# Split-pair projections: five additions into PSUM banks in place of three copies, a join and four additions; evictions read PSUM; order of sums, shifts and loads changed

## The reference

```python
proj = h @ w_in                                   # 1024 x 15 thousand odd columns
branch = jnp.einsum('bsmw,mwd->bsmd', ys, w_branch)
merged @ w_out
u = causal_dwconv(h @ w_up, conv_w, conv_b)       # 3 taps, in front of silu(gate) * value
```

## Time and profile before

| | |
|---|---|
| median of 3 runs | 3483.22 us (3481.16 to 3489.34) |
| the profiled execution | 3483.49 us |
| its span in the profile | 3481.7 us |
| TensorE busy | 3194.5 us, 92% |
| VectorE busy | 1530.1 us, 44% |
| GpSimd busy | 949.2 us, 27% |
| ScalarE busy | 666.8 us, 19% |

### The profile page before, as it was taken

One profiled execution on the slowest core, in us unless ns is written; L12 is line 12 of the kernel. 1 busy time (PEld: TensorE's weight loads), 2 busy tenths in 40 slices (PEclk: granted clock), 3 DMA queues, 4 the chain that ended last, 5 costly groups with the idle time before them and its releaser, 6 DMA issues. The chain is left out here.

```text
span 3481.7 us, 54338 instructions
## 1 busy us (share of the span) xinstructions
PE 3194.5 (92%) x22920; PEld 2164.9 (62%) x22920; DVE 1530.1 (44%) x2308; ACT 666.8 (19%) x1332; POOL 949.2 (27%) x664
## 2 busy tenths in 40 slices
PE   8998999989999789988889999989979986999998
PEld 6855866974887578656555444468758854444432
DVE  4744646135454467445777403554344334011112
ACT  2233141111111333111000001111353211100001
POOL 1201223110222444212999470011365410000000
PEclk9999999998999899999999999989999968999999
DMA  4211223220231000042335342122210013899996
GB/s 156 83 31 41 81 85 103 79 67 0 87 119 49 2 3 4 32 144 74 115 115 156 124 126 66 55 73 73 81 42 3 3 43 133 326 406 409 409 409 256
DMA packets 120560, 406.11 MB, mean 117 GB/s; under 512 B 13824, under 2 KB 18560, under 8 KB 120064
## 3 DMA queue, kind: packets, MB, share of 16 engines
q1 hardware_dynamic: 113408, 377.47, 30.9%
q0 software_dynamic: 6912, 25.17, 2.3%
HBM read 398.39 MB, written 4.19 MB: 116 GB/s over the span
## 5 line engine op out<-in xcount | busy, mean ns | idle before, releaser
L712 PE MATMUL ps<-arena 128*128 128x256 f32 x4592 | 1024.9, 385 | 49.7 <-issue 18.2
L712 PEld LDWEIGHTS ps<-arena 128*128 128x128 f32 x4592 | 883.0, 193 | 202.2 <-issue 64.6
L752 PE MATMUL ps<-arena 128*128 128x512 f32 (+1 forms) x912 | 370.8, 565 | 23.8 <-DVE arena L1047 17.5
L752 PEld LDWEIGHTS ps<-arena 128*128 128x128 f32 x912 | 177.0, 196 | 210.9 <-issue 197.6
L665 POOL TENSOR_TENSOR arena<-arena 128x256 f32<-128x256 f32 x72 | 59.2, 822 | 730.2 <-ACT arena L837 730.2
L3357 PE MATMUL ps<-arena 128*64 128x512 f32 x1024 | 239.3, 602 | 4.9 <-PE ps L3387 2.6
L642 POOL TENSOR_TENSOR arena<-arena 128x512 f32<-128x512 f32 x72 | 92.7, 1287 | 500.6 <-DMA arena<-in_w_in 262.8
L429 PE MATMUL ps<-arena 128*128 128x512 f32 (+1 forms) x416 | 187.5, 611 | 28.8 <-DVE arena L1050 14.9
L837 ACT ACTIVATE arena<-ps 128x256 f32<-128x256 f32 x246 | 92.2, 383 | 586.0 <-PE ps L712 579.2
L3506 POOL TENSOR_SCALAR arena<-arena,small 128x1024 f32<-128x1024 f32 x64 | 188.3, 2942 | 9.3 <-DMA arena<-in_w_mod 5.4
L957 DVE TENSOR_TENSOR arena<-ps,arena 128x256 f32<-128x256 f32 x82 | 34.8, 425 | 351.4 <-PE ps L712 345.1
(11 more groups left out here) (432 smaller groups left out, 4268.1 us busy)
## 6 DMA issues: line engine op xcount, KB each, us to landing
arena<-in_w_in SPq DMA_DIRECT2D x166, 512.0 KB, 3.6
arena<-in_w_gate SPq DMA_DIRECT2D x128, 512.0 KB, 11.2
arena<-in_w_up SPq DMA_DIRECT2D x128, 512.0 KB, 15.0
arena<-in_w_down SPq DMA_DIRECT2D x128, 512.0 KB, 9.1
arena<-in_w_mod POOLq DMA_DIRECT2D x48, 512.0 KB, 4.3
arena<-in_ffn_up SPq DMA_DIRECT2D x44, 512.0 KB, 4.1
arena<-in_w_branch SPq DMA_DIRECT2D x32, 512.0 KB, 3.6
arena<-in_w_out SPq DMA_DIRECT2D x16, 512.0 KB, 3.9
```

The costliest lines, as they stand in the source:

```text
L712: last = nc.tensor.matmul(k.bank(b)[:, 0:HT], lhs[:, q * P:(q + 1) * P], rhs[:, q, :], start=(first and q == 0), stop=(q == 3), skip_group ...
L752: last = nc.tensor.matmul(out[0:j["m"], 0:j["n"]], w[:, q * m:(q + 1) * m], j["rhs"](q), start=(n == 0), stop=(n == kn - 1))
```

## The change

In a pair, only P1 is still copied (into c1). VectorE makes five additions: Q = P6 + P1 into c1; U3 = P7 + Q into c7; C22 = P5 + U3, written into the second half of the bank that P7 holds; C12 = (P5 + P3) + Q, written into the second half of the bank of P1 and P2; C21 = (P7 + P4) + Q, in place. So each job ends as 512 columns of one bank, and `finish` reads PSUM. P3, which TensorE adds to P5, now waits for C22, which reads P5. The join, the copy of C11 and the staging planes go. `finish` of job 0 runs before C21. Banks are handed on after other events: that of P6 after Q, of P5 and P3 after C12, and the two others after the jobs' evictions. ScalarE now evicts its jobs from PSUM in each case, where a plain copy was a no-op.

The order of VectorE: after a split unit's C22, the early sums of the next split unit are made if it is among the next three units, not only if it is the next. In the second block's input phase `finish` and the side step come before the sums, and the four steps of the turn are spread over units 17 to 20. GpSimd makes S1 and S3 of pair after pair with no join between. The shift of a norm is added by ScalarE. The fifteen spare loads are issued at the end of SP's work in the router's phase, behind the following loads.

```diff
-            free += [(b, (k.st_asm, asm0 + 4 * ns + 1)), (a, (k.st_cop, cop0 + 4 * ns + 4)),
-                     (c, (k.st_asm, asm0 + 4 * ns + 2)), (d, (k.st_asm, asm0 + 4 * ns + 3))]
+            free += [(b, (k.st_asm, asm0 + 5 * ns + 1)), (c, (k.st_asm, asm0 + 5 * ns + 4)), (a, jobs[i]["evac"]), (d, jobs[i + 1]["evac"])]
...
     def raw(u, m):
-        j = jobs[u["i"] + m]
-        return j["dst"] if j["eng"] == "A" else k.pl(h.staging[m])
+        return k.bank(u["banks"][("P2", "P4")[m]][0])
...
-                for u in splits:
-                    later = splits[u["s"] + 1] if u["s"] + 1 < ns else None
-                    join(pool, nc.gpsimd, u)
-                    if later:
-                        sum_op(pool, nc.gpsimd, later, "S1", k.st_sump)
-                        sum_op(pool, nc.gpsimd, later, "S3", k.st_sump)
+                for u in splits[1:]:
+                    sum_op(pool, nc.gpsimd, u, "S1", k.st_sump)
+                    sum_op(pool, nc.gpsimd, u, "S3", k.st_sump)
...
-                pe.wait_ge(*copied(u, "P5"))
+                pe.wait_ge(*put_together(u, "C22"))
                 pe.wait_ge(*summed(u, "S4"))
                 halved(u, "P3", plane(u, "S4"), h.x(st, 1, 1), first=False).then_inc(k.piece_done, 1)
-                pe.wait_ge(*copied(u, "P7"))
...
+                for v in units[ui + 1:ui + (4 if u["kind"] == "S" else 2)]:
+                    if v["kind"] == "S" and v["s"] not in summed_units:
+                        later = v
+                        summed_units.add(v["s"])
+                        break
                 if u["kind"] == "C":
+                    if side is not None:
+                        finish(u, 0)
+                        side.dve(dve, u["i"])
+                        if 17 <= ui < 21:
+                            started.add(0)
+                            turn(0, ui - 17)
                     if later:
                         sums_early(later)
                         sums_late(later)
-                    finish(u, 0)
-                    if side is not None:
-                        side.dve(dve, u["i"])
+                    if side is None:
+                        finish(u, 0)
                     continue
...
                 nc.vector.tensor_tensor(h.c1, bank("P6"), h.c1, ALU.add).then_inc(k.st_asm, 1)
+                dve.wait_ge(*put_together(u, "Q"))
+                nc.vector.tensor_tensor(h.c7, bank("P7"), h.c1, ALU.add).then_inc(k.st_asm, 1)
+                dve.wait_ge(*put_together(u, "U3"))
+                nc.vector.tensor_tensor(raw(u, 1)[:, HT:T], bank("P5"), h.c7, ALU.add).then_inc(k.st_asm, 1)
                 if later:
                     sums_early(later)
...
                 nc.vector.tensor_tensor(raw(u, 0)[:, HT:T], bank("P3"), h.c1, ALU.add).then_inc(k.st_asm, 1)
                 if later:
                     sums_late(later)
+                finish(u, 0)
                 dve.wait_ge(*closing(u, "P4"))
                 nc.vector.tensor_tensor(raw(u, 1)[:, 0:HT], bank("P4"), h.c1, ALU.add).then_inc(k.st_asm, 1)
-                if not h.pool:
-                    join(dve, nc.vector, u)
-                dve.wait_ge(*joined(u))
-                nc.vector.tensor_tensor(raw(u, 1)[:, HT:T], h.c1, h.c5, ALU.add).then_inc(k.st_asm, 1)
-                finish(u, 0)
                 finish(u, 1)
...
+                nc.scalar.activation(self.dst(c), self.dst(c), ACT.Identity, bias=self.shift(c)).then_inc(self.ready, 1)
...
             load_following(k, sp, following)
+            if last_loads is not None:
+                last_loads(sp)
...
-    plan(k, spare_slots_phase, k, [MRG_PL + 2 * i for i in range(4)] + [WORK + 36 + 2 * i for i in range(11)])
+    fill_spare = spare_slots(k, [MRG_PL + 2 * i for i in range(4)] + [WORK + 36 + 2 * i for i in range(11)])
...
-         ahead=router_norm)
+         ahead=router_norm, last_loads=fill_spare)
```

More of the change, by code:

```diff
@@ L323, in wtile, with project_phase @@
     return [(w[i, :, a * P:min(a + 8, kt) * P], a, min(8, kt - a)) for a in range(0, kt, 8)]
-def project_phase(k, jobs, following=(), beside=None, moves=(), ahead=None, side=None, halves=None, afterwards=None, tail=None):
+def project_phase(k, jobs, following=(), beside=None, moves=(), ahead=None, side=None, halves=None, afterwards=None, tail=None, last_loads=None):
     if halves is not None:
@@ L529, with __init__ @@
 class Halves:
-    def __init__(self, k, units, sets, sums, copies, staging, pool=True):
+    def __init__(self, k, units, sets, sums, copies, pool=True):
         self.k, self.units, self.sets, self.pool = k, units, sets, pool
-        self.sums, self.staging = sums, staging
-        self.c1, self.c5 = (k.pl(copies[0])[:, n * HT:(n + 1) * HT] for n in range(2))
-        self.c7 = k.pl(copies[1])[:, 0:HT]
+        self.sums = sums
+        self.c1, self.c7 = (k.pl(copies[0])[:, n * HT:(n + 1) * HT] for n in range(2))
     def x(self, s, i, n):
@@ L798, in finish @@
                     if u["kind"] == "S":
-                        act.wait_ge(*(copied(u, "C11") if m == 0 else put_together(u, "C21")))
-                        act.wait_ge(*put_together(u, "C12" if m == 0 else "C22"))
-                        src = j["dst"]
+                        act.wait_ge(*put_together(u, "C12" if m == 0 else "C21"))
+                        src = raw(u, m)
                     else:
@@ L831, in _ @@
                 if u["kind"] == "S":
-                    before = splits[u["s"] - 1] if u["s"] else None
-                    for n, dst, used in (("P1", h.c1, "C22"), ("P5", h.c5, "C22"), ("P7", h.c7, "R")):
-                        act.wait_ge(*product(u, n))
-                        if before:
-                            act.wait_ge(*(joined(before) if used == "R" else put_together(before, "C22")))
-                        nc.scalar.activation(dst, k.bank(u["banks"][n][0])[:, 0:HT], ACT.Copy).then_inc(k.st_cop, 1)
+                    act.wait_ge(*product(u, "P1"))
+                    if u["s"]:
+                        act.wait_ge(*put_together(splits[u["s"] - 1], "C21"))
+                    nc.scalar.activation(h.c1, k.bank(u["banks"]["P1"][0])[:, 0:HT], ACT.Copy).then_inc(k.st_cop, 1)
                 if late is not None:
@@ L842, in _ @@
                 if u["kind"] == "S":
-                    act.wait_ge(*product(u, "P2"))
-                    if js[0]["eng"] == "D":
-                        earlier = [v for v in units if v["kind"] == "S" and v["s"] < u["s"] and jobs[v["i"]]["eng"] == "D"]
-                        if earlier:
-                            act.wait_ge(*jobs[earlier[-1]["i"]]["evac"])
-                    nc.scalar.activation(raw(u, 0)[:, 0:HT], k.bank(u["banks"]["P2"][0])[:, 0:HT], ACT.Copy).then_inc(k.st_cop, 1)
                     late = u
@@ L862, in _, with turn @@
             started = set()
-            def turn(n):
+            def turn(n, only=None):
                 st = h.sets[n]
@@ L893, in finish @@
                 if u["kind"] == "S":
-                    if m == 0:
-                        dve.wait_ge(*copied(u, "C11"))
-                    dve.wait_ge(*put_together(u, "C12" if m == 0 else "C22"))
+                    dve.wait_ge(*put_together(u, "C12" if m == 0 else "C21"))
                     src = raw(u, m)
@@ L1002, in begin @@
     def begin(self):
-        pass
+        if self.shift is not None:
+            self.scaled = self.k.sem(f"norm_scaled{self.base}")
     def sync(self, sp):
@@ L1019, in act @@
         nc.scalar.activation(self.rt, self.inv, ACT.Sqrt).then_inc(self.root, 1)
+        if self.shift is not None:
+            for c in range(KT):
+                act.wait_ge(self.scaled, c + 1)
+                nc.scalar.activation(self.dst(c), self.dst(c), ACT.Identity, bias=self.shift(c)).then_inc(self.ready, 1)
     def square(self, act, c):
@@ L1172, in begin @@
         self.mods_ok = self.k.sem("mods_a_ok")
+        self.first.begin()
     def sync(self, sp):
```

82 lines of the change are left out of this document (35 added, 47 removed).

## The result

The changed kernel takes 3446.56 us (median of 4 runs, 3443.69 to 3448.83) against 3483.8 us of the kernel before beside it; the ratio is 0.9891 [0.9873, 0.9908]. The prediction said 3439, 3422 to 3464. The profiled executions took 3443.69 and 3483.49 us, so 39.8 us are to be found in the traces. First the page of the changed kernel: busy times, then groups (count, busy, mean ns, idle before and what ended it).

A forecast was written before the change was run, and what follows sets the result against it. TensorE, busy 92% of the span, sets the pace in split pairs, so gains lie only where it waits. 35 + 9.5 + 2.5 + 5.8 - 6.5 - 2 = 44.3 us off 3483.2 gave 3439 us, range 3422 to 3464.

The forecast's parts named there:

- the forecast case: Whole kernel: the time lands between 3425 and 3452 us; chance 0.68.
- the margins: Four-tap phases: VectorE's spare time before the next Q is gone, 0.15 us for about 11 pairs, 2 us lost.
- FFN phase: FFN phase: sums made three units ahead close TensorE's holes of 35.8 us; 35 us gained, bounds 22 and 36.
- I price them the same from PSUM: Convolution jobs: the three taps behind the scalar multiply take 2.32 us, whether read from SBUF or PSUM.
- The charge of 0.27 us a job: 70 jobs opening with a scalar multiply: PSUM reads cost VectorE 0.27 us more each, 19 us in all, almost none counted.
- P3 behind C22: Inside pairs: P3 now waits for C22, margin between +0.13 and -0.09 us; no stall taken, at worst 23 us.
- Rival 3: Pairs: C22 late by more than 0.6 us each makes the kernel slower, 3515 us at 1.0 us late; chance 0.05.
- Starts: Seven phase starts: GpSimd's S1 beside the turn stretches the third difference to about 2.3 us; 6.5 us lost.
- Ends: Phase ends: job 0 before C21 and an earlier C22 shorten the uncovered tail; 9.5 us gained.
- Slow clock: Behind waits at phase ends: shorter waits shrink some stretches of lower clock; 2.5 us gained, bounds 0 and 8.
- Second block's input: Second block's input phase: unit 21's job starts 4.3 us earlier, plus 1.5 us of slow clock; 5.8 us gained.
- Shifts and spare loads: Norms and router's phase: shift on ScalarE gains nothing; later loads free the norm but hold the barrier, net nothing.

The follow-up runs named there:

- Experiments 3: Kernel before, with one edit alone: weight sums made for the next split pair up to three units ahead; 3448.31 us, 0.9896.
- 4: Changed kernel without the look-ahead: a split pair's sums made only when it is the next unit; 3445.8 us, 0.9883.
- experiment 5: Kernel before, with seven eighths of GpSimd's work beside the FFN phase left out; 3452.95 us, 0.9902.
- experiment 6: Changed kernel with one more dependent VectorE operation between U3 and C22 in each of the 82 pairs; 3495.79 us, 1.0028.
- experiment 2: Changed kernel, GpSimd waiting before S1 of a phase's second pair until VectorE has made S4 of the first; 3435.45 us, 0.9853.
- experiment 10: Changed kernel with the first job of a pair behind C21 again instead of ahead of it; 3452.49 us, 0.9902.
- experiment 9: Changed kernel with VectorE's old order in whole units of the second block's input phase (turn and sums ahead of unit 21's job); 3448.83 us, 0.9891.
- experiments 11: Changed kernel with the norm's shift back on VectorE behind each scaling; 3445.6 us, 0.9882.
- 8: Changed kernel with the fifteen spare loads issued in a block of their own again, ahead of the router's phase; 3447.1 us, 0.9883.
- experiment 7: Changed kernel with the fifteen spare loads issued by SP ahead of the following loads in the router's phase; 3436.43 us, 0.986.

## Why the prediction was right, and where it was not

The range held and the forecast case came in. That the sum comes within 4.4 us is in part luck: the clock cost 4.1 us against its term and 1.7 more at the starts, and the margins gave back the 2 us charged for them. The median is 7.6 us over the point: 4.4 by the sum of terms (44.3 against 39.9), and 2.9 because the profiled execution was that much faster than its kernel's median, where the one of before was at it.

**FFN phase.** The size of the term was right (35 against 35.8), worked out from the phase's work without holes. The step behind it was right only in part: "the weight sums of this pair are made only after the convolution of the unit just ended" describes the hole, but not why VectorE gets to that job so late. Experiments 3, 4 and 5 each close it, by an earlier place for the sums, by the rest of the change with jobs that read PSUM, and by taking GpSimd's work away. I had priced the job from SBUF on two cheap rows of the first phase, where GpSimd is busy for 27% of the time, against 81% in the FFN phase ("I price them the same from PSUM"). The charge of 0.27 us a job for the read from PSUM came from the same cheap rows. In the FFN phase the job from SBUF costs 1.7 us more than that from PSUM. The group rows of that phase alone, by form, would have shown it.

**P3 behind C22.** Right: no wait, and the margin, put between +0.13 and -0.09, is about 0.04 (experiment 6). Rival 3 was no fancy: 0.64 us more in the chain turned the whole gain into a loss of 0.28%.

**Starts.** The cause was right (experiment 2), the term mis-sized: 8.6 and not 6.5. The third phase alone lost 2.77, of which 1.1 is the third difference. The rest is the clock, and here its place counts more than its length. The third phase by window, before and after:

```profile
374.00:379.00 5.00, 5.00 (x16) 3.79 (x17) 5.00 (x3) 0.38 (x1) 3.34 (x2) 0.66 0.16 66
```

```profile
380.40:385.40 5.00, 3.82 (x10) 3.05 (x11) 1.92 (x4) 0.00 (x0) 0.00 (x0) 0.66 0.00 0
```

Both have 5 us at a mean clock of 0.66. Before, they lie in the turn, where TensorE goes at VectorE's pace in any case, and cost nothing (99.20 us; 99.21 with the clock at 1.00 there in experiment 2). Afterwards they lie behind the longer wait for S2 (2.01 us), where TensorE has all it needs: 5 x 0.34 = 1.7 us. Without it the starts lost 6.9, close to the 6.5. The term had no clock in it, and one trace does not bound that part: merge 3 takes 1.7 to 1.8 us more in four of the other kernels with this start.

**Ends.** Right in kind: 8.8 of 9.5 in this trace, of which 2.7 lie in the two gaps that vary anyway. The job's move is 5.1 (experiment 10).

**Slow clock.** Wrong: "some of these stretches should shrink" failed; I hoped for 2.5 us and lost 1.6. The step that failed is "0.5 x 5.7 = 2.8 us of work lost from the restart on". The retention's input started at a clock of 0.50 for 5.3 us before and at 1.00 in experiment 2, and its stretch is 51.30 and 50.86 us: 0.44 us, not 2.8, because TensorE keeps to the pace of VectorE's turn there, as the prediction itself says of the starts. So there was little to get back. The loss is that of the down projection's start, whose clock got lower behind the same wait; it repeats from kernel to kernel, and what moved it no run here isolates. Together with the 1.7 us in the third phase's start the clock is most of the 4.4: 4.1 here and 2.1 at the starts, against 2 us that VectorE's margin did not cost.

**Second block's input.** Right: 5.5 of 5.8, of which the 4.3 of the wait are safe; the turn spread over four whole units is hidden (experiment 9, by its trace).

**Margins.** The 2 us charged for four-tap phases were not needed: the token-shift phase's stretch with the start mended is 159.65 against 159.63. GpSimd's own work in the FFN phase ended with one operation at 1925.23, 2.35 us long, ahead of the phase's end at 1932: it just fitted.

**Shifts and spare loads.** Both nothing, as predicted (experiments 11 and 8). The prediction saw that the barrier waits for SP's issues, and stopped there; exchanging two lines is worth 10 us (experiment 7).

## What to carry to other kernels

Price an operation in the phase where it runs, and beside what runs there: the same VectorE instruction cost 0.54 us in one phase and 1.19 in another. When a hole closes, test whether the edit that you credit was needed as well as enough; here three different edits each closed it. Look at single records where a mean looks high: here about half of these operations had their usual time, and the others stood still until GpSimd was done. And when issues move behind a queue's waiting one, look at what they then hold up; ahead of the waiting one they were free.

## What the runs showed of the hardware

- VectorE beside a busy GpSimd: operations with SBUF sources went from 543, 692 and 751 ns to 1190, 1496 and 1571 on average; those with a PSUM source and the same width stayed at 750 to 810. The 20 longest of the operations of 512 columns (2.7 to 2.8 us) all started within a GpSimd addition of two SBUF inputs and ended 0.55 us behind it (experiment 5). GpSimd's own 128x512 sum took 1.27 us alone and 2.25 beside VectorE's.
- An addition of 256 columns from PSUM and SBUF into a PSUM bank (C22) took 432 or 433 ns in all 82 pairs, into SBUF (Q) 425 on average.
- The stretches of lower clock move from kernel to kernel in code that is the same: the third and the fourth pair phase took 101.97 and 52.05 us in the changed kernel, 100.29 and 53.73 with the shift moved 1700 us later. The sums, 154.02 and 154.02, are equal. In the eight kernels whose starts have the wait of 2.01 us, leaving out experiment 6, one of the two phases has these 1.7 us; in the five with a wait of 0.94 us or less there, neither has.
- A lower clock costs where the engine has work: 5 us at 0.66 cost nothing in the turn and 1.7 us behind it.
